# Expert blocks of 32 tokens moved as one 4 KB piece per token on 32 partitions, instead of four 1 KB quarters on 128

## The reference: one decoder layer with a hierarchical mixture of experts

```python
def hier_moe(x2, w_rg, b_rg, w_re, b_re, w_e_in, w_e_out):
    # one of 4 groups of experts per token, then the best 2 of its 8 experts
    ...
    gate = g_w[:, None] * e_w / jnp.sum(e_w, axis=-1, keepdims=True)
    expert = (g_idx[:, None] * EXP_PER_GROUP + e_idx).reshape(S).astype(jnp.int32)
    ...
    def expert_block(args):
        xb, e = args
        gu = xb @ w_e_in[e]                 # 1024 -> 2 x 512
        gt, up = jnp.split(gu, 2, axis=-1)
        return (jax.nn.silu(gt) * up) @ w_e_out[e]   # 512 -> 1024
    ...
    y = jnp.sum(out[dest].reshape(T, EXP_TOPK, D_MODEL).astype(f32) * gate[..., None], axis=1)
```

## Time and profile before

| | us |
|---|---|
| median of three runs | 1590.66 |
| the profiled execution's own time | 1599.25 |
| its span | 1597.2 |
| TensorE busy in the span | 1478.5 (93%) |
| VectorE busy | 692.6 (43%) |
| ScalarE busy | 455.4 (29%) |
| GpSimd busy | 187.6 (12%) |
| mean granted TensorE clock | 0.969 |

### The profile page before, as it was taken

How to read it: one execution, slowest core, us unless ns; L and a number is a source line. 1 busy time by engine, 2 the same in 40 slices (tenths; PEclk the granted TensorE clock), 3 DMA queues, 4 the chain that set the end, 5 groups by cost and what they waited for, 6 DMA issues and landing times.

```text
span 1597.2 us, 34713 instructions
## 1 busy us (share of the span) xinstructions
PE 1478.5 (93%) x14399; PEld 1190.5 (75%) x14399; DVE 692.6 (43%) x1246; ACT 455.4 (29%) x870; POOL 187.6 (12%) x360
## 2 busy tenths in 40 slices
PE   7999999999999999999999989979987887997896
PEld 7999999999988999999988769754543443443442
DVE  5766576675789472223444325564111111111114
ACT  4533545445322551223343333111100000000001
POOL 1100000000000000000000000003333233333322
PEclk9999999999999999999999989979998998999998
DMA  5232445434558332262455452966999999999994
GB/s 203 67 92 79 129 128 164 135 102 145 171 205 281 104 93 93 80 226 84 128 193 183 178 215 83 402 250 263 419 423 422 422 421 422 380 412 421 420 410 178
DMA packets 87394, 368.26 MB, mean 231 GB/s; under 512 B 14296, under 2 KB 37536, under 8 KB 72800
## 3 DMA queue, kind: packets, MB, share of 16 engines
q1 hardware_dynamic: 81120, 357.37, 59.1%
q0 software_dynamic: 6144, 8.95, 1.6%
HBM read 344.81 MB, written 29.31 MB: 234 GB/s over the span
## 4 chain that ended last, share of the span: by engine, by line
PE 74%; DMA 17%; DVE 4%; ACT 2%; issue 2%; SPq 1%; POOL 0%; POOLq 0%; DVEq 0%; ACTq 0%
PE ps L638 36%; DMA arena<-in_w 16%; PE ps L1104 8%; PE ps L782 6%; PE ps L1123 4%; PE ps L996 3%; PE ps L887 3%; PE ps L869 3%; PE ps L733 1%; PE ps L730 1%; PE ps L919 1%; PE ps L898 1%; PE ps L1088 1%; PE ps L723 1%; PE ps L1164 1%
## 5 line engine op out<-in xcount | busy, mean ns | idle before, releaser
L1104 PE MATMUL ps<-arena,xT 128*32 128x256 f32 x4096 | 254.4, 400 | 66.7 <-DMA arena<-in_w 64.7
L1104 PEld LDWEIGHTS ps<-arena,xT 128*32 128x32 f32 x4096 | 131.7, 115 | 166.3 <-issue 53.9
L1650 DVE TENSOR_TENSOR wl<-raw,wh 128x1024 fp32r<-128x1024 f32 x151 | 183.4, 1222 | 160.5 <-ACT wh L1195 160.1
L638 PE MATMUL ps<-xh,wh 128*128 128x272 f32 x1136 | 244.2, 296 | 4.6 <-DVE wl L1650 3.4
L638 PE MATMUL ps<-xh,wl 128*128 128x272 f32 x1136 | 235.5, 289 | 0.0
L638 PE MATMUL ps<-xl,wh 128*128 128x272 f32 x1136 | 235.0, 288 | 0.0
L638 PEld LDWEIGHTS ps<-xh,wh 128*128 128x128 f32 x1136 | 179.6, 189 | 15.4 <-issue 9.7
L638 PEld LDWEIGHTS ps<-xl,wh 128*128 128x128 f32 x1136 | 179.2, 189 | 0.0
L638 PEld LDWEIGHTS ps<-xh,wl 128*128 128x128 f32 x1136 | 178.1, 189 | 0.0
L1195 ACT ACTIVATE wh<-raw 128x1024 fp32r<-128x1024 f32 x151 | 158.1, 1055 | 40.4 <-PE ps L996 20.8
L2337 DVE TENSOR_TENSOR hbuf<-sg,ps 128x128 f32<-128x128 f32 x64 | 18.4, 288 | 301.0 <-ACT sg L1502 218.1
(11 more groups left out here) (428 smaller groups left out, 2352.3 us busy)
## 6 DMA issues: line engine op xcount, KB each, us to landing
arena<-in_w SPq DMA_DIRECT2D x96, 2048.0 KB
raw<-in_slabs SPq DMA_DIRECT2D x151, 512.0 KB, 4.4
bc<-acs_dram SPq DMA_DIRECT2D x16, 512.0 KB, 5.8
hs<-in_h SPq DMA_DIRECT2D x16, 512.0 KB, 5.2
out_h_sample<-hs SPq DMA_DIRECT2D x16, 512.0 KB, 4.1
kv<-in_kT SPq DMA_DIRECT2D x8, 1024.0 KB, 4.9
kv<-in_vc SPq DMA_DIRECT2D x4, 1024.0 KB, 7.8
kvx<-in_vc SPq DMA_DIRECT2D x2, 2048.0 KB, 11.9
```

Of the source, the lines that this page charges most:

```text
L638: r = nc.tensor.matmul(ps[:, 2 * (ub % 2) + half, 0:HT], w[:, s, col], x[:, koff + kk, half * HT:half * HT + HT], start=first and kk == 0 ...
L1104: r = nc.tensor.matmul(ps[QS * c:QS * c + QS, 2, 0:2 * FQ], xT[:, s, kk % 2, kk // 2 * QS:kk // 2 * QS + QS], arena[:, at_:at_ + 2 * FQ], ...
L1650: v.tensor_tensor(wl[:, s], raw[:, s], wh[:, s].bitcast(F32), ALU.subtract).then_inc(w_lo, 1)
```

## The change

Each token of a block is now one row of 1024 values (4 KB) on one partition, and a block takes 32 partitions.

- The row numbers count tokens and pairs, no longer quarters; `indices` makes them in two instructions. The scratch tensors are seen as rows of 1024 values, and a gather or a scatter has 32 row numbers.
- `xg` is one tile of 128 x 1024; the block with s = n mod 4 has the partitions 32s to 32s + 31. It is set to zero in one instruction, which waits for the end of the first layer norm, since it lies over one of that norm's rows.
- `turn_x` has eight transposes of 32 partitions x 128 columns, each giving 128 x 32. (The ninth, over the whole tile, is only in the branch that isn't taken.)
- `yb` has the partitions 32s to 32s + 31 with s = n mod 2 for its 1024 values, so `y_copy` has four copies, each of 32 partitions x 256, from partition 32c to 32s.
- `blkeq` moves onto `inblk`, and the product is formed in place.

The core of the diff:

```diff
-        xg = [place(f"xg{i}", [P, QD], F32, at_) for i, at_ in enumerate((e0, e0 + 1024, r_hi + 4 * W1S, r_hi + 4 * W1S + 1024))]
-        yb = place("yb", [P, 2, QD], F32, e0 + 2048)
-        xT = place("xT", [P, 2, 2, P], F32, e0 + 4096)
+        xg = place("xg", [P, D], F32, e0)
+        yb = place("yb", [P, D], F32, st_at)
+        xT = place("xT", [P, 2, KT, QS], F32, e0 + 4096)
...
-        blkeq = place("blkeq", [P, 2 * TT, NBLK], F32, st_at)
+        blkeq = place("blkeq", [P, 2 * TT, NBLK], F32, tmp_at + 8 * TT * P)
...
-                for half in range(2):
-                    r = nc.tensor.transpose(ps[:, 0, half * P:half * P + P], xg[s][:, half * P:half * P + P], ident)
+                rows_ = slice(QS * s, QS * s + QS)
+                if i is not None:
+                    nc.tensor.transpose(ps[:, 3, 0:P], xg[:, 0:P], ident)
+                for kk in range(KT):
+                    r = nc.tensor.transpose(ps[:, 0, kk * QS:kk * QS + QS], xg[rows_, kk * P:kk * P + P], ident[rows_, rows_])
                 r.then_inc(Z["xT_mm"], 1)
...
-                        r = nc.tensor.matmul(ps[QS * c:QS * c + QS, 2, 0:2 * FQ], xT[:, s, kk % 2, kk // 2 * QS:kk // 2 * QS + QS],
+                        r = nc.tensor.matmul(ps[QS * c:QS * c + QS, 2, 0:2 * FQ], xT[:, s, kk],
...
-            for x_ in xg:
-                p_.done(nc.gpsimd.memset(x_[:], 0.0))
+            pool.wait_ge(Z["ln_add"], TT)
+            p_.done(nc.gpsimd.memset(xg[:], 0.0))
...
-                nc.gpsimd.indirect_dma_start(out=xg[s][:], out_offset=None, in_=A["x1d"],
-                                             in_offset=bass.IndirectOffsetOnAxis(ap=gidx[:, s:s + 1] if cnt is None else curg[:, s:s + 1],
-                                                                                 axis=0),
-                                             bounds_check=NQ * T - 1, oob_is_err=False).then_inc(Z[f"g_in{s}"], 16)
+                rows_ = slice(QS * s, QS * s + QS)
+                nc.gpsimd.indirect_dma_start(out=xg[rows_], out_offset=None, in_=x_rows,
+                                             in_offset=bass.IndirectOffsetOnAxis(ap=(gidx if cnt is None else curg)[0:QS, s:s + 1], axis=0),
+                                             bounds_check=T - 1, oob_is_err=False).then_inc(Z[f"g_in{s}"], 16)
...
-                nc.gpsimd.indirect_dma_start(out=A["ybuf"], out_offset=bass.IndirectOffsetOnAxis(ap=curs[:, s:s + 1], axis=0),
-                                             in_=yb[:, s], in_offset=None, bounds_check=2 * NQ * T - 1, oob_is_err=False
+                rows_ = slice(QS * s, QS * s + QS)
+                nc.gpsimd.indirect_dma_start(out=y_rows, out_offset=bass.IndirectOffsetOnAxis(ap=curs[0:QS, s:s + 1], axis=0),
+                                             in_=yb[rows_], in_offset=None, bounds_check=2 * T - 1, oob_is_err=False
...
-                do(v.tensor_scalar(pairi[:, a:b], tab, float(SKIP), None, ALU.add))
-                do(v.tensor_scalar(pairi[:, a:b], pairi[:, a:b], 1, None, ALU.logical_shift_right))
-                v.tensor_scalar(gidx[:, a:b], pairi[:, a:b], float(NQ), cst[:, C_QUAD:C_QUAD + 1], ALU.mult, ALU.add).then_inc(Z["gi_v"], 1)
-                c_.done(v.tensor_scalar(vidx[:, a:b], tab, float(NQ), cst[:, C_SKIP:C_SKIP + 1], ALU.mult, ALU.add))
+                do(v.tensor_scalar(vidx[:, a:b], tab, float(SKIP), None, ALU.add))
+                v.tensor_scalar(gidx[:, a:b], vidx[:, a:b], 1, None, ALU.logical_shift_right).then_inc(Z["gi_v"], 1)
...
-                v.tensor_copy(yb[:, s], ps[:, 5, 0:QD]).then_inc(Z["y_v"], 1)
+                for c in range(NQ):
+                    r = v.tensor_copy(yb[QS * s:QS * s + QS, c * QD:c * QD + QD], ps[QS * c:QS * c + QS, 5, 0:QD])
+                r.then_inc(Z["y_v"], 1)
```

More of the change, by code:

```diff
@@ L278, in build @@
         ovt, eidt = small_tile("ovt", [P, NOV + 1], I32), small_tile("eidt", [P, 1], I32)
-        vidx, gidx, pairi = (small_tile(n_, [P, NBLK], I32) for n_ in ("vidx", "gidx", "pairi"))
+        vidx, gidx = (small_tile(n_, [P, NBLK], I32) for n_ in ("vidx", "gidx"))
         curg, curs = small_tile("curg", [P, 4], I32), small_tile("curs", [P, 2], I32)
@@ L1496, in x_copy @@
                     act.wait_ge(Z["gu_mm"], ix(n_ - 1, i, k))
-                nc.scalar.activation(xT[:, s].rearrange("p h q -> p (h q)"), ps[:, 0, 0:2 * P], ACT.Copy).then_inc(Z["xT_v"], 1)
+                nc.scalar.activation(xT[:, s].rearrange("p k q -> p (k q)"), ps[:, 0, 0:KT * QS], ACT.Copy).then_inc(Z["xT_v"], 1)
             def silu(n_, i=None, k=0):
@@ L1559, in _ @@
             p_ = Count(pool, pool_c)
+            x_rows = A["x1d"].rearrange("(t c) d -> t (c d)", c=NQ)
+            y_rows = A["ybuf"].rearrange("(t c) d -> t (c d)", c=NQ)
             pool.wait_ge(w_free, RING + DENSE)
-            for x_ in xg:
-                p_.done(nc.gpsimd.memset(x_[:], 0.0))
+            pool.wait_ge(Z["ln_add"], TT)
+            p_.done(nc.gpsimd.memset(xg[:], 0.0))
             p_.sync()
@@ L1617, in _ @@
                     pool.sem_inc(Z["on"], 1)
-                    nc.gpsimd.indirect_dma_start(out=xg[1][:], out_offset=None, in_=A["x1d"],
-                                                 in_offset=bass.IndirectOffsetOnAxis(ap=curg[:, 1:2], axis=0),
-                                                 bounds_check=NQ * T - 1, oob_is_err=False).then_inc(Z["g_in1"], 16)
+                    nc.gpsimd.indirect_dma_start(out=xg[QS:2 * QS], out_offset=None, in_=x_rows,
+                                                 in_offset=bass.IndirectOffsetOnAxis(ap=curg[0:QS, 1:2], axis=0),
+                                                 bounds_check=T - 1, oob_is_err=False).then_inc(Z["g_in1"], 16)
                     pool.wait_ge(Z["y_v"], ix(NB0 + 2, ob, 1))
@@ L1624, in _ @@
                     pool.sem_inc(Z["on"], 1)
-                    nc.gpsimd.indirect_dma_start(out=A["ybuf"], out_offset=bass.IndirectOffsetOnAxis(ap=curs[:, 1:2], axis=0),
-                                                 in_=yb[:, 1], in_offset=None, bounds_check=2 * NQ * T - 1, oob_is_err=False
+                    nc.gpsimd.indirect_dma_start(out=y_rows, out_offset=bass.IndirectOffsetOnAxis(ap=curs[0:QS, 1:2], axis=0),
+                                                 in_=yb[QS:2 * QS], in_offset=None, bounds_check=2 * T - 1, oob_is_err=False
                                                  ).then_inc(Z["sc_out1"], 16)
```

## The result

The changed kernel takes 1621.43 us (median of 6 runs, 1618.9 to 1625.15), the kernel before 1592.97 us (median of 6). The ratio is 1.0176 [1.0159, 1.0193]: slower, by 28 us where 20.6 were forecast. 1621.4 lies inside the range, just under its upper end of 1622, and inside the main case's own.

What follows compares the result with a forecast made beforehand. The prediction took full DMA engines moving weights as the bound; 9.3 + 10.6 + 1.9 - 3.0 + 1.0 + 0.8 = +20.6 us on 1590.66 gave 1611 us, with an 8-in-10 range of 1589 to 1622 us.

Steps and rivals of the forecast that it cites:

- main case: Weight stream: narrow 4 KB pieces and weights disturb each other on full DMA engines; 1611 us, own range 1599 to 1624, chance 0.60.
- sign of the main case: Full stretch of the changed profile: DMA share of 1.0 at about 400 GB/s instead of 421.
- The pieces' own length: Gathers and scatters in the stream: 4 KB pieces on 32 partitions take longer, +9.3 us for gathers, +1.9 for scatters.
- The weights held up: Weight transfers beside the gathers: slowed by pieces written to the same partitions, +10.6 us, bounds 0 and 10.6.
- Absorbed: DMA engines in the stream: part of the delays doesn't reach the end, since only the last engine counts, -3.0 us.
- the six-block expert: Expert of six blocks: five longer turns delay the next free slot by 2.5 us, only about +1.0 of it new.
- The turn: TensorE's transposes in each block: eight narrow ones take 0.87 us instead of 0.37, +0.5 us a block.
- The start: Before SP's first weight issue: longer first turns, less shorter index and gather work, +0.8 us, bounds -0.4 and +1.6.
- The copies at the end: Last block: four copies delay the scatter and SP's loads, covered by TensorE's own part, 0 us, bounds 0 and 1.2.
- Rival 1: Stream: transfers don't disturb each other, leaving only the start and the whole six-block expert; 1594 us, chance 0.22.
- Rival 2: DMA engines: a block's rows are dealt so that the 16 carry more equal loads, faster; 1584 us, chance 0.08.
- Rival 3: Gathers and scatters go to eight engines: 1607 us if only scatters do, 1619 if gathers too; chance 0.10.

Runs made afterwards that it cites:

- g_blind: The changed kernel with its narrow transposes turning constants, so gathered tokens are unused; gathers still write 32 neighbouring partitions: 1623.2 us, ratio 1.0175.
- g_spread: The changed kernel with each gather's 32 pieces written to every fourth partition and the transposes turning constants: 1597.98 us, ratio 1.0028.
- g128_s32: The kernel before with only the scatter and the four copies as changed; gather and turns as before: 1598.66 us, ratio 1.0025.
- narrow8: The kernel before with eight narrow transposes instead of two wide ones, gathers and scatters as before: 1596.87 us, ratio 1.0025.
- g32_s128: The changed kernel with the scatter and the single copy to `yb` as before; gather and turns as changed: 1620.9 us, ratio 1.0186.
- copies4: The kernel before with a block's output copied by four instructions of 32 partitions instead of one of 128: 1595.03 us, ratio 1.0012.
- dealt: The kernel before with one table constant changed, dealing a block's slots out over the partitions instead of filling from the front: 1592.0 us, ratio 0.9983.
- list_own: The changed kernel, fixed full list, constants turned, gathers one at a time; 128-row lists, 96 skipped, the rest on every fourth partition: 1703.94 us.
- list_spread: The changed kernel, fixed full list, constants turned, gathers one at a time; 32-row lists written to every fourth partition: 1625.92 us.

## Why the prediction was right, and where its sum was wrong

- **What bounds: right.** The DMA engines are full (1.01) from 1105 to 1385 us in both kernels, and the GB/s fell to the 400 that was named as the sign of the main case. That the gathers' place is what does it, g_blind against g_spread shows.
- **The pieces' own length (+9.3 and +1.9): wrong.** I took the 298 against 161 ns of stores and loads that stand alone. In the stream 4 KB went from 179 to 191 ns: 12 ns x 2176 / 16 = +1.6 us. q0's share rose from 4.6 to 4.8% (the earlier trace rows and the view above), not toward 6.5%. The scatter's part is nothing: g128_s32 kept 421 GB/s. A lone transfer to 32 partitions is slow by itself; in a full stream the same pieces pass at nearly their old price.
- **The weights held up (+10.6): the mechanism was right, the size half.** 30 ns more per 16 KB, over the 182.5 MB of the 29 experts whose weights stream, are 182.5 MB / 16 KB x 30 ns / 16 = +20.9 us. That is twice the upper bound: I had let a piece hold up no more than its own 156 ns of one engine, but it is 20.9 x 16 / 1088 = 307 ns for each gathered piece, as a mean of this kernel. Own pieces and weights together are 22.5 us where 21.8 were written: the sum came out because two errors cancelled, which is luck. g_blind against g_spread gives about 23 us for both, by the place alone.
- **Absorbed (-3.0) and the six-block expert (+1.0): their sum was about right.** The stretch from SP's first issue to the last `down` grew by 17.3 us in the two profiles and by 21.0 in the means of five and five, so of 22.5 + 1.0 us between 2.5 and 6.2 didn't reach the end. Neither term was measured by itself.
- **The turn: too dear.** 0.62 us instead of the forecast 0.87. The eight wide transposes of the earlier trace rows, at 109 ns each, were the wrong row to scale from; narrow ones follow one another at 77 ns. I had said that the loading of 128 columns sets the pace. A single such load isn't shorter in the narrow turn (median 137 ns, against 141 in the wide one), so that reason is wrong too, and what does set the pace stays open. Five turns in the six-block expert make 5 x 0.25 = 1.2 us, not 2.5. Alone, narrow8 cost 0.25%, which is more than the start and that expert explain; where the rest of it lies stays open.
- **The start (+0.8): 0.** The first turn took 1.05 us instead of 0.69 and the second 0.68 instead of 0.44, but a gather was issued in 0.91 us instead of 1.00, and SP's first issue came 30.95 us behind the router's first operation instead of 31.01:

```profile
1076.46 1.05 PE L1091 MATMUL ps<-cst,xg 32*128 32x32 f32 x8 [2.36 <-DMA xg<-x_dram,gidx]
1083.32 0.68 PE L1091 MATMUL ps<-cst,xg 32*128 32x32 f32 x8
1088.34 0.88 SPq L553 DMA_DIRECT2D arena<-in_w  x2
```

- **The copies at the end (0): right.** At the last block TensorE waits for them behind a `down` with no `gate_up` to cover it:

```profile
1572.38 1.71 DVE L2352 COPY yb<-ps 32x256 f32<-32x256 f32 x4 [1.22 <-PE ps L1126]
1574.12 0.29 DVE L2345 COPY hTb<-ps 128x128 f32<-128x128 f32 x1
1574.47 1.93 PE L1126 MATMUL ps<-arena,hTb 128*32 128x256 f32 x32 [1.99 <-DVE hTb L2345]
```

  1.71 us of copies instead of 0.42 stand in front of the copy that `down` needs. That looks like 1.3 us, but the weights were hardly earlier. g32_s128 has the same gathers and one copy, and there `down` waits for the weights:

```profile
1087.54 0.88 SPq L553 DMA_DIRECT2D arena<-in_w  x2
1573.32 1.93 PE L1126 MATMUL ps<-arena,hTb 128*32 128x256 f32 x32 [1.42 <-DMA arena<-in_w]
```

  That is 485.8 us behind SP's issue, against 486.1 with four copies. The last block's own four copies delay its scatter and SP's load, and TensorE's own part covers that, as the prediction said.
- **The end of the program (not in the sum): +6.3.** This is the term that was missing, put at nothing because no row showed it, and it is most of what lies between the 20.6 us forecast and the 28 measured. All ten kernels that have a gather or a scatter with 32 row numbers close with the wait of 6.5 us, and the four that have none (narrow8, copies4, dealt, the kernel before) with 0.2. In g128_s32 TensorE's program is that of before, so it isn't TensorE's code, though the wait is put down to its queue. Nor are the 32 row numbers shown to be the cause: the same ten kernels also have `yb` and `blkeq` at their new places in memory, which the four don't, and no run has one without the other. The profile shows no instruction there, and what makes it stays open. Neither a view of before nor a bound of mine could have given it.
- **The rivals.** Rival 1 (no disturbance, 1594 us) falls with the 400 GB/s, though it would have been right for the scatter. Rival 2 had perhaps a real loss in view, as dealing gained 0.17% in the kernel before; but the change doesn't deal the slots out, and no gain is seen in it. Rival 3 (eight engines carry the pieces) doesn't fit: with q0's 5.9% on eight engines the other eight would have 5.9% to spare and the mean share would lie near 0.95, and it is 1.01 in the full stretch. This is argued from a mean; no view here shows single engines. By it, what is narrow is the place that the gathers write, not the set of engines that carry them.
- **The range.** The main case's own range doesn't follow from its terms to the microsecond: half of the gathers' terms off gives 1601 us and not 1599, and the upper end comes to 1623 and not 1624.

## What to carry to other kernels

Where a stream of weights keeps the DMA engines full, ask of each small transfer beside it where in the partitions it writes, and not only how long its pieces are: the same 4 KB pieces cost nothing that can be told over all 128 partitions and about 23 us of 1594 on 32 neighbours, or on 64 of one half. (No run here gathers over all 128 partitions with 4 KB pieces and uses the tokens; g_spread shows the price of the transfers, not a finished remedy.) A price taken from a transfer that stands alone told that something was narrow, but not who pays: 298 ns alone were 191 in the stream, and the weights beside it, 95% of the bytes, lost 20.9 of the 22.5 us. And a sum that meets the total is not yet right: two of my terms were off by about 10 us each, in opposite directions, and only the time per piece of each queue showed it. The wait at the end was in no term at all.

## What the runs showed of the hardware that I had not expected

- Writing to 32 neighbouring partitions beside a full stream slows the stream's own packets (622 to 652 ns per 16 KB) as well as the narrow pieces (179 to 191 ns per 4 KB, far from the 298 of a lone store). Reading from 32 partitions for the scatters slowed neither (g128_s32: 421 GB/s, 622 and 179 ns).
- The ten kernels with an indirect transfer of 32 rows close 6.3 us later than the four whose lists all have 128 rows, once per program (one profile each, without an exception). The ten also share the new places of `yb` and `blkeq`, so the cause is open.
- A list of 128 rows of which 96 are skipped cost about 1.2 us a gather more than one of 32 rows with the same pieces, where each gather waits for the one before (list_own against list_spread).
- A weight load of TensorE over 128 columns takes as long from 32 partitions as from 128 (137 and 141 ns in the median), and yet eight narrow transposes take 0.62 us and eight wide ones 0.87.
